# Query tiles outermost in attention, with w_out and h2 tile by tile among the steps, and two u tiles in its tail

## What is computed

```
mix = concat(neighbourhood attention (8 heads), HGRN2 recurrence (4 heads), memory attention (4 heads))
x   = x + mix @ w_out
h2  = rmsnorm(x, ffn_norm_g)
# PEER: queries from h2, top 16 of product keys, softmax gates, then
a   = gelu(h2 . u[expert]);  y = sum(a * gate * v[expert]);  x = x + y
out = rmsnorm(x, final_norm_g)
```

## Time and profile before

| | us |
|---|---|
| median of 3 runs | 1797.3 (1796.71 to 1798.61) |
| the profiled execution | 1802.38 |
| its span | 1800.6 |
| attention's steps | 231.2 to 298.0 |
| w_out and h2 | 298.1 to 363.7 |
| routing | 364.0 to 671.1 |

### The profile page before, as it was taken

How to read it: one execution, slowest core, us unless ns; L and a number is a source line. 1 busy time by engine, 2 the same in 40 slices (tenths; PEclk the granted TensorE clock), 3 DMA queues, 4 the chain that set the end, 5 groups by cost and what they waited for, 6 DMA issues and landing times. The chain is left out here.

```text
span 1800.6 us, 32343 instructions
## 1 busy us (share of the span) xinstructions
PE 1714.4 (95%) x11464; PEld 1419.1 (79%) x11464; DVE 1041.7 (58%) x2279; ACT 778.6 (43%) x1268; POOL 861.5 (48%) x713
## 2 busy tenths in 40 slices
PE   6989889989999989999988999999999999999997
PEld 5876644479999989999986877878878778778785
DVE  2766673338787848888444554554554555545544
ACT  5344465243333345555443443444444434434443
POOL 2363230046878770000036665655666666565563
PEclk9989989989999999999999999999999999999999
DMA  4311140044444565777788999999999999999997
GB/s 178 123 64 48 48 188 1 0 164 161 163 163 149 172 197 163 255 254 254 260 285 297 323 345 328 332 340 328 332 341 328 334 337 329 335 335 333 333 316 249
DMA packets 170580, 426.90 MB, mean 237 GB/s; under 512 B 24192, under 2 KB 75520, under 8 KB 170368
## 3 DMA queue, kind: packets, MB, share of 16 engines
q1 hardware_dynamic: 119536, 272.87, 44.8%
q0 software_dynamic: 45056, 134.38, 21.0%
q10 hardware_dynamic: 5904, 18.56, 2.6%
HBM read 389.69 MB, written 36.04 MB: 236 GB/s over the span
## 5 line engine op out<-in xcount | busy, mean ns | idle before, releaser
L1837 POOL DMA_INDIRECT rows<-in_peer_v,row_i x252 | 250.7, 995 | 241.8 <-PE psum L2031 174.5
L1821 POOL DMA_INDIRECT spot<-acts_first,spot_i x256 | 274.2, 1071 | 84.2 <-issue 77.4
L2004 PE MATMUL psum<-h2hi,u_hi 128*128 128x256 f32 x1024 | 293.3, 286 | 2.8 <-PEq L1476 2.8
L2004 PE MATMUL psum<-h2lo,u_hi 128*128 128x256 f32 x1024 | 290.1, 283 | 0.0
L2004 PE MATMUL psum<-h2hi,u_lo 128*128 128x256 f32 x1024 | 289.5, 283 | 0.0
L2004 PEld LDWEIGHTS psum<-h2hi,u_hi 128*128 128x128 f32 x1024 | 194.9, 190 | 58.0 <-issue 32.4
L2014 PE MATMUL psum<-v_hi,w_hi 128*128 128x512 f32 x512 | 202.6, 396 | 2.9 <-DVE w_lo L1916 2.9
L1865 ACT ACTIVATE gel<-psum 128x256 f32<-128x256 f32 x128 | 49.3, 385 | 357.0 <-PE psum L2004 357.0
L2014 PE MATMUL psum<-v_hi,w_lo 128*128 128x512 f32 x512 | 203.3, 397 | 0.0
L2014 PE MATMUL psum<-v_lo,w_hi 128*128 128x512 f32 x512 | 202.8, 396 | 0.0
L1910 DVE TENSOR_TENSOR wgt<-gel,g_in 128x256 f32<-128x256 f32 x128 | 54.6, 427 | 252.8 <-ACT gel L1865 252.8
(11 more groups left out here) (254 smaller groups left out, 3769.5 us busy)
## 6 DMA issues: line engine op xcount, KB each, us to landing
u_raw<-in_peer_u SPq DMA_DIRECT2D x256, 512.0 KB, 4.2
v_raw<-in_peer_v SPq DMA_DIRECT2D x128, 512.0 KB, 7.3
acts_first<-gel SPq DMA_DIRECT2D x128, 128.0 KB, 2.6
gates<-chunk ACTq DMA_DIRECT2D x32, 512.0 KB, 2.7
g_in<-gates SPq DMA_DIRECT2D x64, 256.0 KB, 4.5
wring<-in_w_in SPq DMA_DIRECT2D x24, 512.0 KB, 3.6
wq_raw<-in_w_query SPq DMA_DIRECT2D x16, 512.0 KB, 4.9
w_out<-in_w_out SPq DMA_DIRECT2D x1, 4096.0 KB, 17.3
```

Of the source, the lines that this page charges most:

```text
L1821: pool.indirect_dma_start(spot[:, t:t + 1], None, spots, bass.IndirectOffsetOnAxis(ap=spot_i[:, t:t + 1], axis=0)).then_inc(s_spot, 16)
L1837: pool.indirect_dma_start(rows[:, slot, :], None, values, bass.IndirectOffsetOnAxis(ap=row_i[:, t:t + 1], axis=0)).then_inc(s_rows[q % PER ...
L2004: last = pe.matmul(psum[:, ACTS + s % 2, 0:DENSE], a[:, s % 2, k, :], b[:, k, GATHERED:T], start=(k == 0 and a is u_hi and b is h2hi), sto ...
```

## The change

- The query tile is outermost: unit(u) is now (tile, pair, side). Tokens are kept by grid column everywhere behind build_mix: x is read and out written through columns_of, mq and hg_out are stored in that order.
- Each step moves its 128 columns of mixT out by itself, from one bank. Scores have two banks, after the first tile (0 and 1); w_out has two banks of its own.
- w_out of tile t is done in four pieces of 4 matmuls, behind the values of steps 6(t+1) to 6(t+1)+3; the additions follow at offset 4, the scaling at 5, the turned h2 at 6 and 7 (one pair later than the pieces would need), its split at 7 and 8.
- VectorE normalises memory heads too. GpSimd makes the masked bias by kind of query tile, all heads each.
- In the tail ScalarE loads the table of Sqrt early (warm), u tiles 0 to 3 are split, and tiles 0 and 1 multiplied. Routing begins with u tile 2; the queries begin at u tile 3. Gelu of tiles 0 and 1 stands before the issue of keysT.

```diff
+PRESPLIT, PREDONE = 4, 2
+def columns_of(rows, t):
+    return rows.rearrange("(r c) d -> c r d", c=GRID_W)[t * WIN:(t + 1) * WIN]
...
-    S_SLOTS, T_SLOTS, T_LAG, V_LAG = 6, 4, 4, 6
+    S_SLOTS, T_SLOTS, T_LAG, V_LAG = 6, 4, 4, 3
+    TURN_BANK, VALUE_BANK, H2_BANK, PROJ_BANK = 2, 4, 5, 6
+    PIECES = ((4, 5), (0, 1), (2, 3), (6, 7))
+    ADD_AT, SCALE_AT, TURN_AT = 4, 5, 6
...
-            pair, g, side = u // (2 * NT), (u // 2) % NT, u % 2
+            g, pair, side = u // (2 * PAIRS), (u // 2) % PAIRS, u % 2
...
+        def score_bank(u):
+            return (0, 1, PROJ_BANK, PROJ_BANK + 1)[u % 4] if u < 2 * PAIRS else u % 2
+        def splits_at(c):
+            return {STEPS + 1: (0, 1), STEPS + 3: (2,), STEPS + TURN_AT: (3,)}.get(c, ())
+        def tile_at(c, after):
+            t, off = divmod(c - after, PAIRS)
+            return t - 1 if off == 0 and 1 <= t <= NT else None
...
-            sp.dma_start(x_sb[:], dram["x"].rearrange("(n p) d -> p n d", p=P)).then_inc(s_x, 16)
-            sp.dma_start(gain[:], dram["ffn_norm_g"]).then_inc(s_in, 16)
-            sp.dma_start(w_out[:], dram["w_out"].rearrange("(k p) n -> p k n", p=P)).then_inc(s_wo, 16)
+            for n in range(NT):
+                sp.dma_start(x_sb[:, n, :], columns_of(dram["x"], n)).then_inc(s_x, 16)
+                if n == 0:
+                    sp.dma_start(gain[:], dram["ffn_norm_g"]).then_inc(s_in, 16)
+                    sp.dma_start(w_out[:], dram["w_out"].rearrange("(k p) n -> p k n", p=P)).then_inc(s_wo, 16)
...
# ScalarE
+            for c in range(STEPS + TURN_AT + 3):
+                for u in (2 * c, 2 * c + 1):
+                    if u < UNITS:
+                        exps(u)
+                    if T_LAG <= u < UNITS + T_LAG:
+                        move_probT(u - T_LAG)
+                if c == STEPS + 1:
+                    act.activation(warm[:], eps[:], ACT.Sqrt)
+                    act.wait_ge(s_u0, 16 * USLOTS)
+                    act.wait_ge(s_score, UNITS)
+                for n in splits_at(c):
+                    if n == 2:
+                        act.wait_ge(s_pv, STEPS)
+                    act.copy(u_hi_of(n), u_raw[:, n, :, :]).then_inc(s_uhi, 1)
+                parts_at(act, c)
+                t = tile_at(c, ADD_AT)
+                if t is not None:
+                    act.wait_ge(s_x2, 2 * (t + 1) + 1)
+                    act.activation(h2[:, t % 2, :], x_sb[:, t, :], ACT.Square, accum_out=ss[:, t:t + 1]).then_inc(s_sq, 1)
+                    act.wait_ge(s_sq, t + 1)
+                    act.activation(std[:, t:t + 1], ss[:, t:t + 1], ACT.Sqrt, bias=eps[:, 0:1], scale=1.0 / D).then_inc(s_std, 1)
...
# VectorE, in each step c: move_out(c - 4), then for both units maximum,
# reciprocal and product of the unit before, then:
+                t = tile_at(c, ADD_AT)
+                if t is not None:
+                    for half in range(2):
+                        dve.wait_ge(s_proj, 2 * t + half + 1)
+                        dve.tensor_tensor(x_sb[:, t, wide], psum[:, PROJ_BANK + half, :], x_sb[:, t, wide], ALU.add)
+                for n in splits_at(c):
+                    dve.wait_ge(s_uhi, n + 1)
+                    dve.tensor_tensor(u_lo_of(n), u_raw[:, n, :, :], u_hi_of(n).bitcast(F32), ALU.subtract)
+                t = tile_at(c, SCALE_AT)
+                if t is not None:
+                    dve.wait_ge(s_std, t + 1)
+                    dve.reciprocal(rstd[:, t:t + 1], std[:, t:t + 1]).then_inc(s_rstd, 1)
+                    dve.tensor_scalar(h2[:, t % 2, :], x_sb[:, t, :], rstd[:, t:t + 1], None, ALU.mult)
+                parts_at(dve, c)
...
# TensorE
             def scores(u):
-                if u >= 4:
-                    pe.wait_ge(s_max if u - 4 < NA_UNITS else s_exp, u - 3)
+                v = score_user(u)
+                if v is not None:
+                    pe.wait_ge(s_max if is_na(v) else s_exp, v + 1)
...
             def values(c):
                 pe.wait_ge(s_probT, 2 * c + 2)
-                if c % NT == 0 and pair >= 2:
-                    pe.wait_ge(s_out, pair - 1)
+                if c:
+                    pe.wait_ge(s_out, c)
...
+            for c in range(STEPS + TURN_AT + 2):
+                if c < STEPS:
+                    scores(2 * c)
+                    scores(2 * c + 1)
+                if T_LAG <= 2 * c < UNITS + T_LAG:
+                    turn(2 * c - T_LAG)
+                    turn(2 * c - T_LAG + 1)
+                if 0 <= c - V_LAG < STEPS:
+                    values(c - V_LAG)
+                for piece in range(len(PIECES)):
+                    t = tile_at(c, piece)
+                    if t is not None:
+                        project(t, piece)
+                if c == STEPS + TURN_AT:
+                    activations(0)
+                for half in range(2):
+                    t = tile_at(c, TURN_AT + half)
+                    if t is not None:
+                        turn_h2(t, half)
+            activations(1)
...
# routing
+    FIRST_QUERY = 1
         def query_at(n):
-            return n // QEVERY if n % QEVERY == 0 and n // QEVERY < HC else None
+            n -= PREDONE + FIRST_QUERY
+            return n // QEVERY if n >= 0 and n % QEVERY == 0 and n // QEVERY < HC else None
...
+            gelu(0)
+            gelu(1)
             act.dma_start(keysT[:], dram["sub_keys"]).then_inc(s_in, 16)
...
-            for n in range(EARLY_ROUTING):
+            for n in range(PREDONE, EARLY_ROUTING):
                 pe.wait_ge(s_ulo, n + 1)
```

More of the change, by code:

```diff
@@ L929, in _ @@
             sp.wait_ge(s_u0, 16 * USLOTS)
+        PARTS = sorted(mask_parts(), key=lambda part: part[0])
         def masked_of(h, g):
-            _, of, start = next(part for part in mask_parts() if part[0] == (g if g in (0, NT - 1) else 1))
-            return bm[:, h % B_SLOTS, start:start + of.stop - of.start], of
-        def masked_bias(eng, h):
-            for g, of, start in mask_parts():
-                wide = slice(start, start + of.stop - of.start)
-                last = eng.tensor_tensor(bm[:, h % B_SLOTS, wide], keep["spare"][:, wide], bias[:, h, of], ALU.add)
-            last.then_inc(s_bm, 1)
+            return bm[(0, 1, 1, 2)[g]][:, h, :]
@@ L942, in _, with masked_count, masked_bias @@
+        def masked_count(h, g):
+            return (0, 1, 1, 2)[g] * NA_HEADS + h + 1
+        def masked_bias(eng, kind, h):
+            _, of, start = PARTS[kind]
+            wide = slice(start, start + of.stop - of.start)
+            eng.tensor_tensor(bm[kind][:, h, :], keep["spare"][:, wide], bias[:, h, of], ALU.add).then_inc(s_bm, 1)
         @block.gpsimd
         def _(pool):
-            pool.wait_ge(s_bm, 1)
-            masked_bias(pool, 1)
-            for h in range(2, NA_HEADS):
-                if h >= B_SLOTS:
-                    pool.wait_ge(s_max, 2 * NT * ((h - B_SLOTS) // 2) + 2 * (NT - 1) + h % 2 + 1)
-                masked_bias(pool, h)
@@ L952, in turned_h2 @@
[L952 to L960 removed]
+            pool.wait_ge(s_bm, 2)
+            for kind in range(3):
+                for h in range(2 if kind == 0 else 0, NA_HEADS):
+                    masked_bias(pool, kind, h)
@@ L961, in h2_parts, with turned_h2 @@
+        def turned_h2(t, k):
+            bank = TURN_BANK if t == NT - 1 and k >= 4 else H2_BANK
+            return psum[:, bank, (k % 4) * P:(k % 4 + 1) * P]
+        def h2_parts(eng, t, half):
+            for k in range(4 * half, 4 * half + 4):
+                src, c = turned_h2(t, k), slice(t * P, (t + 1) * P)
                 if eng is nc.scalar:
+                    if k % 4 == 0:
+                        eng.wait_ge(s_hT, 2 * t + half + 1)
                     eng.activation(h2hi[:, k, c], src, ACT.Identity, scale=gain[:, k:k + 1]).then_inc(s_hi, 1)
@@ L1002, in _ @@
-            act.wait_ge(s_in, 16)
-            for i in range(NT):
-                if i:
-                    h2_parts(act, i - 1)
-                act.wait_ge(s_x2, 2 * (i + 1) + 1)
-                act.activation(h2[:, i, :], x_sb[:, i, :], ACT.Square, accum_out=ss[:, i:i + 1]).then_inc(s_sq, 1)
-                act.wait_ge(s_sq, i + 1)
-                act.activation(std[:, i:i + 1], ss[:, i:i + 1], ACT.Sqrt, bias=eps[:, 0:1], scale=1.0 / D).then_inc(s_std, 1)
-            h2_parts(act, NT - 1)
+                act.copy(probT[:, u % T_SLOTS, 0:w], psum[:, TURN_BANK + u % 2, 0:w]).then_inc(s_probT, 1)
@@ L1110, in values @@
                             v = mv[:, kt, h * HD:(h + 1) * HD]
-                        last = pe.matmul(psum[rows(side), 6 + pair % 2, g * P:(g + 1) * P], v,
+                        last = pe.matmul(psum[rows(side), VALUE_BANK, 0:P], v,
                                          probT[:, (2 * c + side) % T_SLOTS, j * P:(j + 1) * P],
```

261 lines of the change are left out of this document (137 added, 124 removed).

## The result

The changed kernel takes 1806.98 us (median of 6 runs, 1805.56 to 1813.54), the kernel before 1797.37 (6 runs, 1796.71 to 1800.21). The ratio is 1.0057, with a 95% interval of 1.0041 to 1.0074: slower by about 10 us, where 1795 and no difference were forecast. The profiled execution of the changed kernel took 1805.71 us, its span is 1803.6.

A forecast was written before the change was run, and what follows sets the result against it. TensorE, busy 95% of the span, was taken as the bound, through idle time and half clock. Attention +9.1, block end 0, routing -8.6 - 2.1 - 1.8 + 0.9, stores +0.3 gave -2.2: 1795 us, range 1787 to 1804.

The forecast's parts named there:

- Start of the pieces: Attention's first query tile: w_out lands and the first piece starts at 246 us, bounds 244.5 and 249.5.
- The gaps and what makes them: Attention, after tiles 0 to 2: Sqrt's table switches delay exponentials; TensorE waits 4.15 + 4.15 + 6.1 = 14.4 us.
- TensorE's own work: Attention from the first piece: 38.9 us of attention left, 54.9 of w_out, 2.7 of h2 turns.
- The clock: Attention: half clock after each of three gaps, 1.7 us lost each, 5.1; 0.75 more at the start.
- Table loads without a drain: ScalarE in attention: six added table loads cost 1.29 us each, without the skill's 1.38 us drain per switch.
- From the last piece to the end of the block: Attention's end: the same chain stands there as before, so 8.0 us again.
- w_query: Routing's start: w_query 0 lands at 4 rather than 6.1 us, -2.1; query 0 at +7.5 us.
- Routing: Three fewer u tiles later, -8.6 us; half clock at query 0 gone, -1.8; GpSimd's remainder late, +0.9.
- (a): Three gaps in attention: clock stays up and gaps are a microsecond shorter each; 1790 to 1787 us, chance 0.36.
- (b): Three gaps in attention: half clock lasts 10.2 us after each in place of 3.4; +10.2, 1805 us, chance 0.19.
- (c): ScalarE stands still behind each table switch for as long again as the load; +7.7, 1803 us, chance 0.06.
- (d): Attention: nothing is overlapped, pieces wait for w_out or mixT in every tile; chance 0.01.

The follow-up runs named there:

- the control: Changed kernel with the root of query tiles 0 to 2 on VectorE, plus four extra matmuls at step offset 5 of tiles 0 to 2: 1797.2 us.
- with the gaps filled: Changed kernel with four extra, unused matmuls in each of TensorE's three gaps, table loads kept: 1798.33 us.
- with the root out of the way: Changed kernel with the root of tiles 0 to 2 on VectorE and the tail's splits of u tiles 0 and 1 later: 1790.63 us.
- the late split: Changed kernel with the tail's splits later, u tile 0 by one step and tile 1 by two, tile 2 as before: 1804.84 us.

## Why the prediction was wrong

I take the steps of the forecast in turn.

**Start of the pieces.** Forecast at 246, 14.8 us after the first scores; measured 15.8 (228.56 to 244.38). +1.0.

**The gaps and what makes them.** Right in kind and place: three gaps, each ended by ScalarE's exponential or the probT copy behind it, two table loads ahead. The waits were put at 4.15 + 4.15 + 6.1 = 14.4 and are 3.48 + 3.41 + 4.07 = 11.0, with 1.6 more of short waits inside the rows of scores behind the first two. -1.8. The tail's was put at 2.4 and is 2.27.

**TensorE's own work.** This is the first of the two steps that failed, and the larger one. The forecast added 38.9 for attention left, 54.9 for w_out and 2.7 for the turned h2, 96.5 in all; the control shows 101.7. +5.2. A piece was put at 8 x 0.429 = 3.43, from a run of 12 passes in the midst of w_out. Between values and scores it takes 3.63 (244.38 to 248.01), and in the control the 128 passes take 58.0 us: +3.1, the price of cutting w_out into pieces, for which the sum had no term. The width of the neighbours alone doesn't make it: in the kernel before, eight passes behind eight turns of h2, of 128 columns, take 3.43.

```profile
319.71 3.60 PE L1144 MATMUL psum<-w_out,mixT 128*128 128x512 f32 x8
323.14 1.02 PE L1144 MATMUL psum<-w_out,hg_out 128*128 128x512 f32 x2
```

The turned h2 is 0.6 more (24 at 0.14, not 0.11), and attention left is 1.5 more. Nearly all of that last part is in three rows of memory scores that take 1.05, 1.05 and 1.42 us where 0.63 was counted (267.87, 305.06 and 338.27 in the changed kernel, and the same in the control); in the third, the profile shows the second unit's weights waiting 0.50 us for the exponential that frees one of the two banks. The sum took scores at the pitch that they have with four banks.

**The clock.** This is the second step that failed: "3.4 us of it where TensorE has a piece to do: 1.7 us lost each, 5.1", and 0.75 at the start. The half clock behind gaps was foreseen but mis-sized. It lasted 6.8 us, not 3.4, behind two of the three gaps. It came behind the tail's wait of 2.27 too, for which I had none. And it lay almost wholly on TensorE's path: the scores, turns and values in the gap's shadow, which I had treated as thin work that waits anyway, run in sequence ahead of the next piece. Of the 20.4 us, 18.9 have TensorE at work, which loses half of them, 9.4; at the start nothing was lost. Against 5.85 that is +3.6. For the three gaps alone it is 7.75 against 5.1, and filling them gave back 6.7 to 8.0, which is the same term seen from the other side.

These are +1.0 - 1.8 - 0.1 + 5.2 + 3.6 = +7.9, where the table above has 7.5; 0.4 stays unassigned. Waits and clock of the three gaps together were forecast at 19.5 and come to 20.3. So the loss at the table loads was in the sum at nearly its full price; what made the forecast miss is TensorE's own work, and half clock in the tail.

**Table loads without a drain.** Right. By the Trainium skill ("ScalarE: Activation LUTs", What ACT_TABLE_LOAD costs) 1380 ns of drain go with each switch. Here Sqrt starts 1.30 us after its load starts and the exponential 1.30 after its own (272.16, 273.46), so the drain is no part of these rows. That the page's rule would have given 1803, on the right side of the forecast, is no point for the mechanism.

**From the last piece to the end of the block.** 8.0 forecast, 7.6 measured (369.94 to 377.56). **w_query:** query 0 at 8.5 us in the block, 7.5 forecast. I had keysT issued behind the table load and two Gelu; it is issued at 377.65, at once, since the issuing part of ScalarE doesn't stand behind them in this trace. w_query's first part so landed beside it and was split from 4.96 us in the block, where 4 was forecast and 6.1 was the time before. +0.6 for the two together. The 2.17 us that the first u tile waits for Gelu cost query 0 nothing, as w_query came later still.

**Routing.** Three u tiles fewer behind query 0, and no half clock at its start: -7.8 measured, -9.5 forecast. Near 642 TensorE waits 2.39 us for GpSimd's remainder of a u tile, which stands behind the two products of 635.30 to 640.01 on GpSimd, and 3.4 us of half clock follow from 644. The wait itself is not new: the kernel before has it too.

```profile
630.46 0.39 PE L1425 MATMUL psum<-h2hi,u_hi 128*128 128x256 f32 x1 [1.79 <-POOL u_lo L1315]
```

With the new token order alone it is 1.86, and in the traces of the changed kernel and its variants 1.79 to 2.67. No half clock follows it in the first two; in both executions of the changed kernel 3.4 us do, in some variants none. So a part of the missing 1.7 us is here: 0.6 of wait and up to 1.7 of clock.

**The rivals.** (a), clock up and shorter gaps, at 1787 to 1790: false for this change, and nearly its time once the root leaves ScalarE (1791.6); with the gaps filled its part on the clock holds, in a kernel of 1798.3. (b), long half clock, at 1805: its mechanism made a part of the miss, at 6.8, 3.4 and 6.8 us and not 10.2. That its price is nearest to the measured time is luck: behind the three gaps the clock cost 2.65 us more than forecast, not 10.2, and TensorE's own work made up the most of the rest. No rival had that. (b) was given 0.19, and deserved more: its rows were the nearest ones in kind, thin work at the start of attention, while I leaned on a gap with full work behind it. (c) is false, (d) too.

**Did the change do what it says?** Yes. The idle and half-clock time of attention's steps was to be filled with w_out, and with the root out of the way it is: 1790.6, and 122.6 us in the stage. What was gained there was given back by moving Sqrt among the exponentials of the same engine.

## What to carry to other kernels

Before work of one stage is interleaved into another, look at which table sets its ScalarE functions need: table loads on a queue that feeds TensorE cost here nearly twice their own time (13.6 to 14.7 us for six loads of 1.29), since the engine that waits also comes back at half clock. A small function such as the root of 128 numbers can go to VectorE, in 2.5 us that lie beside a matmul. And price a gap as its wait and its clock together, with all work behind it in the clock's part; a run with harmless work in the gap, and the same work where there is no gap, tells the two shares apart. Last, when long work is cut into pieces, take the pitch of a piece from rows where it stands between its new neighbours, and the pitch of those from rows with as few banks as they will have: here this was worth more than the clock.

## What was not expected of the hardware

Waits of 3.48 and 4.07 us were followed by 6.8 us at half clock, one of 3.41 by 3.4, one of 2.27 by 3.4. With the root on VectorE a wait of 0.44 was followed by none. Waits of 1.04 and 0.32 in the third place were followed by none there, but by 3.4 us with the late split added; and the tail's wait of 2.3 was followed by none in the control with filler. The length of a wait alone doesn't tell what follows it, and what does is not shown here. A run of eight 512-column passes takes 3.63 us between values and scores, in the changed kernel and as filler alike, 3.43 behind turns of h2 in the kernel before, and 3.43 by the pitch in the midst of such passes. Useless work of 10.9 us made a kernel 8.0 us faster.
